# A hybrid layer with 32 experts on one core: 2 KB of descriptor scratch for 16, SiLU and its product in one buffer, two more down weights resident, expert 1's rows turned behind expert 0

## What is computed

```python
g_idx = top_k(softmax(t @ router_group_w + b), 1)      # 4 groups
e_top = top_k(expert logits inside the group, 2)        # 8 experts per group, 32 in all
hg = einsum("td,edf->tef", t, exp_w_gate)               # 1024 -> 256
hu = einsum("td,edf->tef", t, exp_w_up)
hid = silu(hg) * hu * combine[:, :, None]
out = einsum("tef,efd->td", hid, exp_w_down)            # 256 -> 1024
h = layer_norm(alpha * h + out)
```

## Time and profile before

| | |
|---|---|
| three timed executions | 448.27, 449.0, 450.28 us (median 449.0) |
| the profiled execution, its own time | 447.62 us |
| its span, first to last instruction | 445.8 us |
| mean granted clock of TensorE | 0.977 of full |
| PE busy | 412.4 us (93%) |
| bytes moved by the DMA engines | 139.10 MB |

### The profile page before, as it was taken

The page is one execution under the profiler, slowest core; times in us unless marked ns, Lnnn a source line. Parts: engine busy times, 40 slices in busy tenths (PEclk is TensorE's granted clock), DMA queues, the critical chain, the costliest instruction groups (busy, mean ns, idle before and its releaser), DMA issues.

```text
span 445.8 us, 6662 instructions
## 1 busy us (share of the span) xinstructions
PE 412.4 (93%) x2594; PEld 276.0 (62%) x2594; DVE 187.4 (42%) x375; ACT 114.3 (26%) x185; POOL 83.5 (19%) x112
## 2 busy tenths in 40 slices
PE   7999999999999999889999999999987979787891
PEld 6788877888888888755555555655544435443330
DVE  2659522799954485745222221222211111211085
ACT  4443388942150014101111111111101101111411
POOL 2500000000000001013333223332222123200133
PEclk9999999999999999999999999999989889998996
DMA  8866522022399999789999999999999999998583
GB/s 266 258 176 195 184 94 96 0 94 96 97 346 389 412 420 392 305 297 413 411 407 401 369 410 410 407 410 411 411 410 413 412 414 412 412 415 354 192 326 141
DMA packets 45568, 139.10 MB, mean 312 GB/s; under 512 B 5351, under 2 KB 17671, under 8 KB 41446
## 3 DMA queue, kind: packets, MB, share of 16 engines
q1 hardware_dynamic: 39376, 126.89, 73.5%
q0 software_dynamic: 6144, 11.84, 7.2%
q10 hardware_dynamic: 22, 0.02, 0.0%
HBM read 134.41 MB, written 12.58 MB: 330 GB/s over the span
## 4 chain that ended last, share of the span: by engine, by line
PE 70%; DMA 18%; DVE 6%; SPq 3%; issue 1%; ACT 0%; DVEq 0%; ACTq 0%; POOLq 0%
PE bank L1083 18%; PE bank L904 11%; PE bank L906 11%; PE bank L905 11%; DMA wdn<-in_exp_w_down 10%; PE bank L1102 9%; DMA wgu<-in_exp_w_up 5%; PE bank L1071 2%; PE bank L1093 2%; DMA raw<-in_w_in 2%; PE bank L1157 2%; SPq L503 2%; DMA xg<-h_rows,x_rows 1%; DVE stats L1522 1%; PE bank L1011 1%
## 5 line engine op out<-in xcount | busy, mean ns | idle before, releaser
L1083 PE MATMUL bank<-wgu,xTg 128*64 128x256 f32 x960 | 111.9, 386 | 7.1 <-DMA wgu<-in_exp_w_up 6.7
L1083 PEld LDWEIGHTS bank<-wgu,xTg 128*64 128x64 f32 x960 | 67.2, 139 | 42.7 <-DMA wgu<-in_exp_w_up 7.2
L1102 PE MATMUL bank<-wdn,hidT 128*64 128x512 f32 x248 | 61.3, 616 | 8.1 <-DMA wdn<-in_exp_w_down 7.7
L904 PE MATMUL bank<-xT_hi,w_hi 128*128 128x512 f32 x160 | 63.0, 394 | 1.7 <-DVE xT_lo L1206 1.7
L906 PE MATMUL bank<-xT_hi,w_lo 128*128 128x512 f32 x160 | 62.3, 389 | 0.0
L905 PE MATMUL bank<-xT_lo,w_hi 128*128 128x512 f32 x160 | 62.3, 389 | 0.0
L679 POOL DMA_INDIRECT y_pairs<-ys,y_rows x32 | 32.6, 1018 | 146.2 <-PE bank L1071 95.1
L1478 DVE TENSOR_TENSOR hid<-gated,bank 64x256 f32<-64x256 f32 x32 | 13.5, 423 | 104.9 <-ACT gated L839 104.9
L839 ACT ACTIVATE gated<-bank 64x256 f32<-64x256 f32 x32 | 12.1, 379 | 142.2 <-PE bank L1083 142.2
L1183 DVE TENSOR_TENSOR w_lo<-raw,w_hi 128x2048 fp32r<-128x2048 f32 x12 | 27.5, 2288 | 26.9 <-ACT w_hi L753 26.9
L1102 PEld LDWEIGHTS bank<-wdn,hidT 128*64 128x64 f32 x248 | 17.2, 137 | 32.0 <-issue 18.4
(11 more groups left out here) (242 smaller groups left out, 437.2 us busy)
## 6 DMA issues: line engine op xcount, KB each, us to landing
wdn<-in_exp_w_down SPq DMA_DIRECT2D x31, 1024.0 KB, 20.4
wgu<-in_exp_w_gate SPq DMA_DIRECT2D x30, 1024.0 KB, 14.9
wgu<-in_exp_w_up SPq DMA_DIRECT2D x30, 1024.0 KB, 18.4
raw<-in_w_in SPq DMA_DIRECT2D x9, 1024.0 KB, 5.3
raw<-in_w_out SPq DMA_DIRECT2D x4, 1024.0 KB, 5.0
pair_y<-y_pairs SPq DMA_DIRECT2D x8, 512.0 KB, 7.6
xres<-in_x SPq DMA_DIRECT2D x4, 512.0 KB, 7.5
h_rows<-xres POOLq DMA_DIRECT2D x4, 512.0 KB, 7.8
```

Source lines behind the costliest of these rows:

```text
L904: pe.matmul(dst, a_hi, b_hi, start=start, stop=False)
L1083: mm = pe.matmul(psum[2 + b][BLOCK * which:BLOCK * which + BLOCK, 0:F], xTg[b][:, j, h * BLOCK:(h + 1) * BLOCK], wgu[s][:, which, k, :], s ...
L1102: mm = pe.matmul(psum[6 + b][BLOCK * n:BLOCK * n + BLOCK, :], hidT[b][:, j, :], wdn[s][:, j, n * H:(n + 1) * H], start=j == 0, stop=j == 1)
```

## The change

- The descriptor scratch at the start of SBUF, from which POOL's DMAs take their descriptors, is 2 KB per partition instead of 16 KB. Three waits are added among POOL's small loads at the start.
- SiLU writes to the upper 64 partitions of `hid`, and the product writes to the lower 64. The two `gated` buffers (1 KB each) go, and so do the two memsets of `hid` and the wait for them. `turn_hid` multiplies only the lower 64 partitions with a 64x64 identity instead of transposing 128x128.
- Two more buffers for down weights, `wdn_extra`; they take experts 7 and 8, whose loads are issued right behind expert 0's. Down weights thus have nine places at first instead of seven.
- `refill_gu` no longer runs two experts ahead of `refill_dn` in SP's order.
- Expert 1's rows are turned after expert 0's `gate_up`, not in its middle.
- The router's product waits for each half of a turned tile; the first half of tile 3 is turned ahead of router 2.

```diff
-DN_FIRST = RING + 1
+DN_FIRST = RING + 3
...
+        wdn += [at(f"wdn_extra{b}", [P, 2, D], F32, spare + 16384 + 8192 * b) for b in range(2)]
...
             load_gu(0, 0, gu_in[0])
             load_dn(0, 0, dn_in[0])
+            load_dn(RING + 1, RING + 1, dn_in[RING + 1])
+            load_dn(RING + 2, RING + 2, dn_in[RING + 2])
             sp_.wait_ge(y_lo_ready, KT)
...
-            LEAD = 2
...
-                refill_gu(q + LEAD, 0)
+            for q in range(DN_FIRST, DN_FIRST + RING):
+                refill_gu(q, 0)
                 refill_dn(q, 0)
...
+            pool.wait_ge(gates_in, 32)
+            pool.wait_ge(ln1_in, 32)
             pool.dma_start(wr[:, :, 0:N_GROUPS], router_group_w.rearrange("(k p) n -> p k n", p=P)).then_inc(router_in, 16)
+            pool.wait_ge(router_in, 16)
...
-                pool.memset(hid[b][:, :], 0.0).then_inc(hid_zero, 1)
...
-                act.activation(gated[b][:, :], psum[2 + b][0:BLOCK, 0:F], ACT.Silu).then_inc(gated_ready, 1)
+                act.activation(hid[b][BLOCK:, :], psum[2 + b][0:BLOCK, 0:F], ACT.Silu).then_inc(gated_ready, 1)
...
+            turn_h1(TT - 1, (0,))
             router(TT - 2)
-            turn_h1(TT - 1)
+            turn_h1(TT - 1, (1,))
...
-                    cols = hid[b][:, :].rearrange("p (m j) -> p j m", j=2)[:, j, :]
-                    mm = pe.transpose(psum[4 + b][:, j * P:(j + 1) * P], cols, ident[:, :])
+                    cols = hid[b][0:BLOCK, :].rearrange("p (m j) -> p j m", j=2)[:, j, :]
+                    mm = pe.matmul(psum[4 + b][:, j * BLOCK:(j + 1) * BLOCK], cols, ident[0:BLOCK, 0:BLOCK], start=True, stop=True)
...
-                gate_up(q + r * RING, gu_slot(q), q % 2, 2, gu_loads(q, r),
-                        amid=(lambda: turn_main_x(1, 0)) if q == 0 else None)
+                gate_up(q + r * RING, gu_slot(q), q % 2, 2, gu_loads(q, r))
                 if q == 0:
+
+                    turn_main_x(1, 0)
                     return
...
-                v.tensor_tensor(hid[b][0:BLOCK, :], gated[b][:, :], psum[2 + b][BLOCK:2 * BLOCK, 0:F], ALU.mult).then_inc(hid_ready, 1)
+                v.tensor_tensor(hid[b][0:BLOCK, :], hid[b][BLOCK:, :], psum[2 + b][BLOCK:2 * BLOCK, 0:F], ALU.mult).then_inc(hid_ready, 1)
...
-    nc = _bacc.Bacc("TRN2", target_bir_lowering=False, num_devices=1)
+    nc = _bacc.Bacc("TRN2", target_bir_lowering=False, num_devices=1, dynamic_dma_scratch_size=2048)
```

More of the change, by code:

```diff
@@ L163, in hybrid_moe_layer @@
         xTg = [sb(f"xTg{b}", [P, 4, P]) for b in range(2)]
-        gated = [sb(f"gated{b}", [BLOCK, F]) for b in range(2)]
         hid = [sb(f"hid{b}", [P, F]) for b in range(2)]
@@ L437, in dn_loads @@
         def dn_loads(q, r):
-            return r + (1 if q < DN_FIRST else (q - 1) // RING + 1)
+            return r + (1 if q < DN_FIRST else (q - 3) // RING + 1)
         def rounds(engine, body):
-            head, turns = GU_FIRST, (N_EXP - 1 - GU_FIRST) // RING
+            head, turns = DN_FIRST + 1, (N_EXP - 1 - (DN_FIRST + 1)) // RING
             for q in range(head):
@@ L548, in refill_dn @@
                 load_dn(q + r * RING, dn_slot(q), dn_in[dn_slot(q)])
-            LEAD = 2
-            head = GU_FIRST + RING - LEAD + 1
-            turns = (N_EXP - LEAD - head) // RING
+            turns = (N_EXP - DN_FIRST - RING) // RING
             refill_gu(GU_FIRST, 0)
-            for q in range(DN_FIRST, head):
-                refill_gu(q + LEAD, 0)
+            for q in range(DN_FIRST, DN_FIRST + RING):
+                refill_gu(q, 0)
                 refill_dn(q, 0)
@@ L559, in _ @@
                 for u in range(RING):
[L560 to L570, removed]
+                    refill_gu(DN_FIRST + RING + u, r)
+                    refill_dn(DN_FIRST + RING + u, r)
+            for q in range(DN_FIRST + RING + turns * RING, N_EXP + 1):
+                if q < N_EXP:
+                    refill_gu(q, 0)
+                if q > DN_FIRST + RING + turns * RING:
+                    refill_dn(q - 1, 0)
             last_of_1 = max(q for q in range(N_EXP) if gu_slot(q) == 1)
@@ L662, in _ @@
                 pool.dma_start(h1_rows[2 * t * P:2 * (t + 1) * P, :].rearrange("(p a) h -> p (a h)", a=2), xres[:, t, :]).then_inc(h1_stored, 16)
-            pool.wait_ge(routed, TT)
-            for b in range(2):
-                pool.memset(hid[b][:, :], 0.0).then_inc(hid_zero, 1)
             pool.wait_ge(xg_zero, ROWS - 1)
@@ L991, in _, with turn_h1 @@
                 pe.wait_ge(w_lo_ready, c + 1)
-            def turn_h1(t):
+            def turn_h1(t, halves=(0, 1)):
                 if t >= 2:
                     pe.wait_ge(h1T_ready, 2 * (t - 1))
-                for n in range(2):
+                for n in halves:
                     pe.wait_ge(h1_ready, 2 * t + n + 1)
@@ L1072, in turn_x, with gate_up @@
                 mm.then_inc(xg_turned, 1)
-            def gate_up(i, s, b, lag, loads, amid=None):
+            def gate_up(i, s, b, lag, loads):
                 pe.wait_ge(gu_in[s], 32 * loads)
@@ L1078, in gate_up @@
                 for k in range(KT):
-                    if amid and k == KT // 2:
-                        amid()
                     h, j = divmod(k, 4)
@@ L1428, in _ @@
                     v.tensor_scalar(x_rows[:, 0:N_EXP], psum[1][:, 0:N_EXP], half_no_row, None, ALU.add).then_inc(rows_ready, 1)
-            v.wait_ge(hid_zero, 2)
             copy_xT(0, 0, 2)
```

23 lines of the change are left out of this document (12 added, 11 removed).

## The result

The changed kernel takes **444.19 us** (median of four executions, 444.09 to 444.76) against 448.87 us for the kernel before on the same chip (four executions, 448.27 to 450.28). The ratio is 0.9894, with a 95% interval of 0.9869 to 0.9919. That is 4.7 us faster, where 6.5 were forecast. The profiled execution took 444.16 us, its span is 442.4, its mean clock 0.99; against the profiled execution of before (447.62, span 445.8) that is 3.4 to 3.5 us, since that one was 1.25 us quicker than its median.

What follows compares the result with a forecast made beforehand. The weight stream was taken as the bound: bytes left over 411 GB/s plus DMA holes. Early down weights 5.10 us plus PE's 1.4 us make 6.5 us, so 449.0 - 6.5 = 442.5 us, range 440.2 to 446.5.

Steps and rivals of the forecast that it cites:

- first three holes: Stretches at 134 to 136, 186 to 191 and 195 to 199 us with idle DMA engines: 6.85 us missing, to close.
- Two down weights early: Two 1.05 MB loads behind expert 0's at 126.17 us fit into holes; the last weights land 5.10 us earlier.
- The block at 244.2 us: Expert 14's load waits for expert 8's `gate_up` with the queue empty; PE 1.4 us early ends this at about 244.2 us.
- turn_hid: PE's turning of hid as a 64-column product takes 0.34 us for 0.44: 0.1 us saved per expert, 0.8 over eight.
- SP's order at nothing: Expert 16's gate and up stand behind expert 15's waiting down weights: at worst 1.4 us once, taken as nothing.
- The smaller scratch at nothing: The smaller descriptor scratch for POOL's DMAs was taken to cost or save nothing in the steady state.
- Router order: With tile 3's first half turned ahead, the last router ends 0.3 us earlier, between nothing and 0.55.
- Expert 1's rows: Turned behind expert 0's `gate_up`, they let expert 1 start 0.3 us earlier; bounds 0.65 saved, 1.75 lost.
- Rival 1: The first gather waits for the early loads' backlog, expert 1 starts 1.75 us later: 444.6 us; chance 0.12.
- Rival 2: Only bytes count: hid's turning no shorter, or SP's order opens a 1.4 us hole; 443.9 to 444.9 us; chance 0.16.
- Rival 3: More of PE's bursts in the last experts run at 1.2 GHz, 1.5 us each; three make 447.0 us; chance 0.06.
- Rival 4: Scratch too small, gather and scatter one after the other, 13.3 us per expert, over 640 us; with unseen stalls, chance 0.06.

Runs made afterwards that it cites:

- e3: The changed kernel without the two early down weights and with SP's order of before: 448.28 us, ratio 0.9999 to the kernel before.
- e2: The changed kernel with SP's gate and up loads one expert ahead again behind expert 15: 442.65 us, ratio 0.9874 to the kernel before.
- e1: The changed kernel with hid turned by two 128x128 transposes again: 440.76 us, ratio 0.9828 to the kernel before.
- e4: The changed kernel with both 128x128 transposes and gate and up loads one expert ahead behind expert 15: 441.13 us, ratio 0.9824 to the kernel before.
- e9: The kernel before with only the 2 KB scratch and POOL's three waits: 447.36 us against 448.86, ratio 0.996.
- e8: The changed kernel with 128x128 transposes, gate and up loads one expert ahead behind expert 15, and loops written out: 440.39 us, ratio 0.9805.
- e12: The changed kernel with transposes, all places used in turn, PE kept busy, each gate-and-up pair ahead of the previous expert's down weights: 440.11 us, ratio 0.9806.
- e6: The changed kernel with all eight gate-and-up and nine down places used in turn, loops written out, SP's order by trigger time: 442.06 us.

## Why the prediction was right in size, and where its steps were not

By spans, before to after: -6.9 us in the first three holes, -0.4 us of an earlier start of the stream (122 to 134 us, where the 14 profiles differ by up to 2.2 us, whatever the kernel), +0.4 at 201 to 241, +3.6 at the block, +2.4 at the second hole. These make -0.9 us, and h1 in fact lands 1.1 us earlier. The silence at the end: -2.0. The rest, -0.3, holds the last `gate_up` at full clock, of which the later steps gave most back. So -1.1, -2.0 and -0.3 make the -3.4 us.

The total lies in the range, but the forecast's mechanism had the last weights 6.5 us earlier, at 398.7 us, and they land 1.1 us earlier, at 404.07. Its own signs tell the same: a hole did open near 258 us, which it had named as a sign of being wrong; the block ends at 247.86 for 244.2; the period is 6.61 us for 6.14; and from the start of expert 31's `gate_up` to the end it is 38.3 us, not 40.6. That the total came out is in part luck. Held were the closing of the first three holes, expert 8's load at 193.78 and expert 1's start at 195.87.

- **Two down weights early, 5.10 us: held.** The holes close as the forecast said, with expert 8's earlier load 6.85 us in all. e3 against e2 measures it, 5.6 us in time and 5.1 us of missing time; against the changed kernel e3 loses only 4.1 us (4.7 by the ratios), since with SP's order of before it has hardly any second hole.
- **The block at 244.2 us: wrong by 3.66 us** (247.86). The queue did run dry near 244 us. The mechanism (what PE gains until then counts fully) was right, and it worked against the change.
- **turn_hid, 0.1 us saved per expert: wrong in sign, and the step that failed.** It costs 0.37 us per expert. "Four such rows are 0.22 us" priced moving columns at `gate_up`'s pace, where weight loads have 64 columns. The measured 0.61 lies above even the upper bound of 0.48, and neither bound looked at the loads of the instruction behind, where the other 0.20 us are. Eight times 0.37 is 3.0 us lost before the trigger, where 0.8 were to be won and 0.3 lost at worst. e1 measured the step: 3.4 us by the medians, 3.0 by the ratios.
- **SP's order at nothing: wrong by 2.4 us**, above its own bound of 1.4. The step counted on a period of 6.24 us and on gathers to cover the gap; two periods of 6.61 put the down load at 262.80, 14.9 us after the block's end. With 14.9 in the forecast's own sum, 1.1 us without work and a start-up of 1.05, the hole comes to 2.2 us. So most of this miss follows from `turn_hid`. e2 took the hole away and won 1.5 us of the median, 1.7 of the span. With the period at 6.24 the load comes 14.2 us after the block's end, as worked out, and e1 still shows 0.96 us of missing time there, within the bound of 1.4 and not nothing.
- **The smaller scratch at nothing: wrong by 2.0 us, in the other direction.** No row of before prices it; the silence of 2.5 us could have been read in that profile, but not that it hangs on the scratch. It hid a third of the losses above.
- **Router order, 0.3 us: measured nothing.** The second half's copy is still what the last router waits for: from the start of the last normalization to the router's end 4.45 us pass (172.54 to 176.99), before it was 4.46 (172.95, to 177.41).
- **Expert 1's rows, 0.3 us: held in the changed kernel, 0.4.** Expert 1 starts 0.78 us earlier, of which 0.41 were there already at the last normalization (172.54 for 172.95). In e1 and e4 the gain is eaten by the wait for expert 2's rows. Timeline of the kernel after:

```profile
194.18 0.75 PE L1069 MATMUL bank<-ident,xg 128*128 128x128 f32 x4 [0.44 <-DMA xg<-h_rows,x_rows]
195.87 3.67 PE L1079 MATMUL bank<-wgu,xTg 128*64 128x256 f32 x32 [0.94 <-DVE xTg L1411]
```

- **Rival 1 (the gather behind the backlog) is out:** issue to landing of the first gather is 6.16 to 6.52 us in the ten profiles with the early weights, against 6.09 to 6.38 in the four without. "DMA: Bandwidth & Descriptors" in the Trainium skill, section "Queues, rings and completion order", says that each DMA engine takes its queues in turn, a packet at a time; the trace agrees. Rival 2's hole came, though bigger. Rival 3 did not: of the last two `gate_up`s one is at the level of 1.2 GHz (expert 30's, 5.36 us), as before (expert 31's, 5.11). Rival 4 is out: the stream of 270 to 385 us runs at 411 GB/s as before, and e9 is no slower.

In the forecast's account the holes shrink from 7.9 us to 1.4; by the windows they shrink from 8.4 to 7.8. Of the 6 us between, 3.5 are the block, 2.4 the second hole. Against them stand 2.0 us of scratch, 0.4 of earlier start and half a microsecond of smaller things: 3.1 us short on the profiled pair, and 1.7 on the medians (444.19 for 442.5), since the forecast's scale put 1.4 us on top for the quick profile of before. A right total, then, with two large errors one way, the second mostly a consequence of the first, and a smaller, unseen one the other way.

The changed kernel with the old transposes and the loops written out, with its loads in e2's order (e8) or with the places used in turn and PE kept busy (e12), takes 440.4 and 440.1 us: 1.9% less than the kernel before, while the change as made takes 1.1% less.

## What to carry to other kernels

When a stream of loads sets the end, keep one account: bytes over the steady rate, plus each stretch's missing time. Here it followed the landing of the last load to within 1.6 us over 14 kernels. A faster or slower engine counts only where a place is waited for with the queue empty; give such places back in turn and its pace stops mattering. Price a small product by its weight loads as well as by its moving columns, and look at what happens between the last byte and the end: a setting that touches no instruction may sit there.

## What the hardware showed that was not expected

- A 64x64 plain float32 product costs more than a 128x128 transpose: 0.61 against 0.44 us for a pair, and 0.2 us more for the transposes behind it.
- The descriptor scratch, 16 KB for 2 KB, costs 2.0 us after the last byte of the kernel in the profiles (2.5 us for 0.5), with nothing in the trace; e9's timed gain of 0.23% to 0.56% agrees.
- The queue does not end at once. In e6 SP issues nothing between the load of h1, at 386.47 us, and two loads of 0.5 MB each at 399.31 and 399.70, yet the rate falls off over ten microseconds until h1's landing at 409.5:

```profile
399.31 0.34 SPq L567 DMA_DIRECT2D ln2g<-in_ln_g  x1
399.70 0.43 SPq L568 DMA_DIRECT2D ln2b<-in_ln_b  x1
...
398.00:404.00 6.00, 3.97 (x21) 1.94 (x19) 0.30 (x2) 0.60 (x1) 0.99 (x1) 0.80 0.90 352
404.00:406.00 2.00, 2.00 (x16) 1.29 (x14) 0.00 (x0) 0.00 (x0) 0.00 (x0) 0.74 0.61 245
406.00:408.00 2.00, 2.00 (x16) 0.86 (x12) 0.42 (x1) 0.38 (x1) 0.00 (x0) 1.00 0.42 174
408.00:410.00 2.00, 1.57 (x10) 0.77 (x8) 0.29 (x1) 0.60 (x1) 0.02 (x1) 1.00 0.28 115
```

The DMA share falls with the rate, from 0.90 to 0.28. That reads as some DMA engines being through long before others, with the load landing on the slowest, but the share is a mean over all 16, so it is not shown. The Trainium skill, "DMA: Bandwidth & Descriptors", section "Latency and other measured facts", says that engines 7 and 15 are usually slower in traces; the cause that it guesses at lies with the DMAs of POOL, and these loads are SP's. No row here tells the engines apart. An estimate from the four rows: their 3.2 MB at 411 GB/s would be through 4 us sooner. Whether an even split is to be had stays open.
